# Retention's rotary half-swap: four ScalarE copies between partition halves in place of two matmuls with a constant matrix

## What is computed

```python
def apply_rotary(t, cos, sin):
    t1, t2 = jnp.split(t, 2, axis=-1)
    return jnp.concatenate([t1 * cos - t2 * sin, t1 * sin + t2 * cos], axis=-1)

def retention_mixer(q, k, v, cos, sin):
    q = apply_rotary(q.astype(f32), cos, sin)
    k = apply_rotary(k.astype(f32), cos, sin) * HEAD_DIM ** -0.5
    ...
```

## Time and profile before

| | us |
|---|---|
| median of 3 runs | 3160.13 |
| lowest and highest run | 3157.06 and 3163.06 |
| span of the profiled execution, first to last instruction | 3158.7 |
| TensorE busy in it | 3088.7 (98%) |
| VectorE busy | 1326.2 (42%) |
| ScalarE busy | 909.1 (29%) |
| GpSimd busy | 262.5 (8%) |

### The profile page before, as it was taken

The page is one execution under the profiler, slowest core; times in us unless marked ns, Lnnn a source line. Parts: engine busy times, 40 slices in busy tenths (PEclk is TensorE's granted clock), DMA queues, the critical chain, the costliest instruction groups (busy, mean ns, idle before and its releaser), DMA issues.

```text
span 3158.7 us, 35787 instructions
## 1 busy us (share of the span) xinstructions
PE 3088.7 (98%) x14698; PEld 2538.4 (80%) x14698; DVE 1326.2 (42%) x1417; ACT 909.1 (29%) x995; POOL 262.5 (8%) x275
## 2 busy tenths in 40 slices
PE   7999999999999999999899999999999999999998
PEld 5778777777789988887688888888888888888886
DVE  4534656555344442422324343334334343433335
ACT  6322433333344332322223212222221212122222
POOL 3000111100001123100022000000000000000002
PEclk8999999999999999999999999999999999999999
DMA  7333222222336764432433333332333333233332
GB/s 230 89 90 88 64 60 57 56 61 80 106 99 195 229 196 119 138 85 80 120 93 93 94 97 101 96 93 93 93 97 91 104 93 93 93 93 99 92 101 80
DMA packets 499007, 326.48 MB, mean 103 GB/s; under 512 B 12654, under 2 KB 487920, under 8 KB 498160
## 3 DMA queue, kind: packets, MB, share of 16 engines
q1 hardware_dynamic: 487568, 287.52, 32.1%
q0 software_dynamic: 11360, 37.85, 3.2%
HBM read 302.28 MB, written 23.07 MB: 103 GB/s over the span
## 4 chain that ended last, share of the span: by engine, by line
PE 92%; DVE 3%; ACT 3%; issue 1%; DMA 0%; POOL 0%; DVEq 0%; SPq 0%; ACTq 0%; POOLq 0%
PE slab_ps L652 20%; PE slab_ps L654 20%; PE slab_ps L653 20%; PE mix_ps L652 8%; PE mix_ps L654 8%; PE mix_ps L653 8%; PE mix_ps L1088 1%; PE mix_ps L1071 1%; PE mix_ps L821 1%; PE mix_ps L924 1%; PE mix_ps L829 1%; ACT w_hi L1167 1%; DVE w_lo L1650 1%; PE mix_ps L828 1%; PE mix_ps L966 1%
## 5 line engine op out<-in xcount | busy, mean ns | idle before, releaser
L652 PE MATMUL slab_ps<-act_hi,w_hi 128*128 128x512 f32 (+1 forms) x3216 | 1230.5, 383 | 13.4 <-DVE act_lo L2118 6.4
L654 PE MATMUL slab_ps<-act_hi,w_lo 128*128 128x512 f32 (+1 forms) x3216 | 1201.8, 374 | 0.0
L653 PE MATMUL slab_ps<-act_lo,w_hi 128*128 128x512 f32 (+1 forms) x3216 | 1201.5, 374 | 0.0
L1167 ACT ACTIVATE w_hi<-w_raw 128x2048 fp32r<-128x2048 f32 x264 | 505.2, 1914 | 1274.0 <-PE slab_ps L654 695.9
L652 PEld LDWEIGHTS slab_ps<-act_hi,w_hi 128*128 128x128 f32 x3216 | 608.5, 189 | 132.3 <-issue 18.0
L1650 DVE TENSOR_TENSOR w_lo<-w_raw,w_hi 128x2048 fp32r<-128x2048 f32 x264 | 604.7, 2291 | 238.5 <-ACT w_hi L1167 238.3
L654 PEld LDWEIGHTS slab_ps<-act_hi,w_lo 128*128 128x128 f32 x3216 | 607.9, 189 | 107.9
L653 PEld LDWEIGHTS slab_ps<-act_lo,w_hi 128*128 128x128 f32 x3216 | 609.0, 189 | 106.3 <-issue 6.2
L654 PE MATMUL mix_ps<-u_hi,w_lo 128*128 128x512 f32 x1024 | 404.5, 395 | 0.0
L652 PE MATMUL mix_ps<-u_hi,w_hi 128*128 128x512 f32 x1024 | 404.5, 395 | 0.0
L653 PE MATMUL mix_ps<-u_lo,w_hi 128*128 128x512 f32 x1024 | 404.4, 395 | 0.0
(11 more groups left out here) (347 smaller groups left out, 1744.3 us busy)
## 6 DMA issues: line engine op xcount, KB each, us to landing
w_raw<-in_w_mlp_up_dram SPq DMA_DIRECT2D x64, 1024.0 KB, 6.4
w_raw<-in_w_mlp_down_dram SPq DMA_DIRECT2D x64, 1024.0 KB, 5.3
w_raw<-in_w_in_dram SPq DMA_DIRECT2D x56, 1024.0 KB, 5.5
w_raw<-in_w_cross_kv_dram SPq DMA_DIRECT2D x32, 1024.0 KB, 6.3
w_raw<-in_w_mix_out_dram SPq DMA_DIRECT2D x16, 1024.0 KB, 5.9
w_raw<-in_w_cross_q_dram SPq DMA_DIRECT2D x16, 1024.0 KB, 5.9
w_raw<-in_w_cross_o_dram SPq DMA_DIRECT2D x16, 1024.0 KB, 5.9
main<-x_park POOLq DMA_DIRECT2D x8, 1024.0 KB, 6.0
```

What stands on the lines that cost most here:

```text
L652: mm(ps, wh, xh, start=first, stop=False)
L653: mm(ps, wh, xl, start=False, stop=False)
L654: return mm(ps, wl, xh, start=False, stop=last)
L1167: fn(w_hi[:, slot], w_raw[:, slot], ACT.Copy).then_inc(on["slab_hi"], 1)
```

## The change

The matrix `rot`, its set-up on POOL and the two matmuls a head are gone. ScalarE's part of a retention head begins instead with a wait for `slab_out` and four activations of type Copy, 64 partitions by 512 each, from one half of `stage` to the other half of `ret_t`, the one that lands in partitions 0 to 63 with scale -1. Each raises `ret_rot` by one. VectorE waits for the first two before the sine product of q and for all four before that of k, and makes the product in place in `ret_t`, from SBUF. TensorE keeps its waits and starts with the transposes.

```diff
@@ tiles @@
-            rot = sb("rot", [P, P])
@@ gpsimd @@
-            chain.link(nc.gpsimd.memset(rot[:], 0.0))
-            for m0, base, fill in ((0, -CH, -1.0), (CH, 0, 1.0)):
-                half = rot[:, m0:m0 + CH]
-                chain.put(nc.gpsimd.affine_select(out=half, in_=half, compare_op=ALU.not_equal, fill=fill, base=base,
-                                                  pattern=[[-1, CH]], channel_multiplier=1))
@@ tensor: retention(par) @@
-                q, k, v = (stage[:, par, t] for t in range(3))
+                v = stage[:, par, 2]
                 head_starts()
                 pe.wait_ge(on["slab_out"], slabs.at())
-                mm(M[0][:], rot[:], q, start=True, stop=True)
-                mm(M[1][:], rot[:], k, start=True, stop=True).then_inc(on["ret_rot"], 1)
                 turn(M[2], lambda t: v[:, t * P:(t + 1) * P], "vt_ready")
@@ scalar @@
-            def retention():
+            def retention(par):
                 head_starts()
+                act.wait_ge(on["slab_out"], slabs.at())
+                for n in range(2):
+                    fn(ret_t[0:CH, n], stage[CH:P, par, n], ACT.Copy, scale=-1.0).then_inc(on["ret_rot"], 1)
+                    fn(ret_t[CH:P, n], stage[0:CH, par, n], ACT.Copy).then_inc(on["ret_rot"], 1)
                 values(M[2])
@@ vector: retention(par, hd) @@
-                dve.wait_ge(on["ret_rot"], hd + 1)
                 for n, t in enumerate((q, k)):
                     dst = (ret_q, ret_k)[n]
                     chain.put(tt(dst[:], t, cos_t[:], ALU.mult))
-                    chain.link(tt(ret_t[:, n], M[n][:], sin_t[:], ALU.mult))
+                    dve.wait_ge(on["ret_rot"], hd * 4 + (2 * n + 2))
+                    chain.link(tt(ret_t[:, n], ret_t[:, n], sin_t[:], ALU.mult))
```

More of the change, by code:

```diff
@@ L1438, in _ @@
                 for par in range(2):
-                    mixer = retention()
+                    mixer = retention(par)
                     for _ in range(4):
```

## The result

The changed kernel takes **3198.06 us** (median of 4 runs, 3196.38 to 3198.27), the kernel before beside it 3158.6 us (4 runs, 3156.84 to 3163.06). The ratio is 1.0122, with a 95% interval of 1.011 to 1.0134: some 39 us slower, where 7 us less were forecast. The profiled execution took 3198.09 us, its span is 3196.6.

The account below looks back on a forecast made before the run. TensorE was taken to bound the kernel (busy 98%, 92% of the chain). Its -6.9 us, with 0 elsewhere, took the median from 3160.13 to 3153.2 us, range 3149.5 to 3159.0.

Parts of the forecast that it names:

- The step that failed: Stages behind retention: each was to start 6.9 us earlier and keep its shape.
- Removed matmuls, 6.9 us: TensorE in the four retention heads: losing two rotation matmuls saves 1.72 us a head, 6.9 us in all.
- The 3.5 us: Estimate for the removed matmuls' 16 records on TensorE by the skill's rule, about 216 ns each; set aside for measured distances.
- Junction 0: TensorE in retention heads: transposes now directly follow a slab's matmul, opening no gap, at most 0.1 us a head.
- Copies, 0.55 us each: ScalarE in retention heads: four added copies at 0.55 us each, 2.2 us a head, cost on the path 0.
- The cover: ScalarE in the second retention head: copies fit its 2.96 us idle before `vtok`, with 5.75 us idle later as second cover.
- VectorE's waits 0, 4.3 us of slack: VectorE in retention heads: waiting for copies before the sine products costs 0; sums stay 4.3 us ahead of TensorE's scores.
- POOL's set-up and the moved tiles, 0: Dropping POOL's memset and two selects (1.0 us) gains 0; tiles moving 512 bytes a partition without `rot` cost 0.
- C: Retention heads: slow copies hold VectorE's second wait and stop TensorE; at 3.2 us a copy, 3169.7 us; chance 0.03.
- if the stage is 6.9 us shorter and the end is not: Profile sign of a wrong forecast, for A or D; the granted clock behind 307 us was to tell which.
- A: Near delta heads' ends: shifted clock falls; two more in the median give 3156.6 us, two fewer 3149.8; chance 0.22.
- D: Unexamined slack, say in the delta heads, takes the shift back: nothing measurable, 3160 us; chance 0.07.

Follow-up runs that it names:

- e2: Kernel before without the two rotation matmuls a head and their waits, nothing in their place, half-swap left out, `rot` and set-up kept: 3197.9 us, ratio 1.0117.
- e1: Changed kernel with 32 already met waits (16 instructions) on TensorE ahead of the MLP's loop, putting it back to its old place: 3153.78 us, ratio 0.998.
- e4: Kernel before with one turn of the output projection's loop written out and 24 instructions of met waits ahead of the MLP's loop: 3182.56 us, ratio 1.0073.
- e6: Changed kernel with one turn of the cross-attention output projection's loop written out ahead of it, no waits added: 3151.53 us, ratio 0.9973.
- e3: Changed kernel with `rot`, its set-up and its two matmuls a head put back, results unused, VectorE still using the copies: 3161.5 us, ratio 1.0004.
- e7: e1 with 8 instructions of met waits in place of 16, so the MLP's loop starts at 12746: 3153.2 us.
- e8: e4 with 12 instructions of met waits in place of 24, so the MLP's loop starts at 12960: 3179.95 us.
- e10: e6 with 72 met waits (37 instructions) put inside the MLP's loop at its top, body 1615 instructions: 3203.55 us.
- e11: e4 with 36 instructions of met waits in place of 24, so the MLP's loop starts at 12984: 3188.66 us.

## Why the prediction was wrong

**The step that failed** is: "After retention every stage starts 6.9 us earlier and keeps its shape, since its weights are loaded into slots that TensorE and VectorE free." The stages behind retention have the same work and the same waits, but they didn't keep their place in TensorE's instruction stream. The prediction counted the eight matmuls as time where they stood and nothing else; without their 16 instructions the MLP's loop, which makes its first jump at 2069 us, begins ahead of a piece boundary instead of behind it. e2 makes this loss out of the removal alone, e1 takes it back with 16 instructions that do nothing, and e4 brings a loss of the same kind into the kernel before. The bill is -6.9 + 6 x 7.2 = +36, measured +39.

Term by term:

- *Removed matmuls, 6.9 us*: right. The first delta head starts 6.86 us earlier, and e1 (ratio 0.998, so 6.3 us less) and e6 (0.9973) show the gain at the end once the loop stays resident. The 3.5 us that the prediction worked out from the Trainium skill ("TensorE: Matmul & The Clock Gate", section "Back-to-back issue gap") was half of what came.
- *Junction 0*: right, 0.24 and 0.44 us.
- *Copies, 0.55 us each*: too low. The timeline of ScalarE in the second head, after:

```profile
149.18 1.92 ACT L1159 ACTIVATE w_hi<-w_raw 128x2048 fp32r<-128x2048 f32 x1 [8.96 <-PE slab_ps L648]
151.12 0.63 ACT L1288 ACTIVATE ret_t<-stage 64x512 f32<-64x512 f32 x1
151.77 0.63 ACT L1289 ACTIVATE ret_t<-stage 64x512 f32<-64x512 f32 x1
...
153.74 0.60 ACT L1182 ACTIVATE vtok<-mix_ps 128x512 f32<-128x512 f32 x1
...
154.89 0.63 ACT L1169 ACTIVATE gtmp<-gtmp 128x512 f32<-128x512 f32 x1
...
160.55 1.92 ACT L1159 ACTIVATE w_hi<-w_raw 128x2048 fp32r<-128x2048 f32 x1 [4.36 <-PE slab_ps L648]
```

  They start 0.65 us apart, each 0.63 long: as long as a pass of the sigmoid over 128 partitions beside them (L1169), so half the partitions made them no shorter and the way between halves no longer. Four take 2.6 us, where 2.2 was said. The cover was right: they lie in what was idle time ahead of `vtok`. They hold `vtok` back by about 1.5 us behind the transposes (done at about 152.2), as the prediction had it in kind, and nothing waited for it.
- *VectorE's waits 0, 4.3 us of slack*: right, and e3 shows it by itself. Timeline of VectorE there, after:

```profile
154.27 0.69 DVE L1759 TENSOR_TENSOR ret_t<-ret_t,sin_t 128x512 f32<-128x512 f32 x1
...
155.60 0.69 DVE L1759 TENSOR_TENSOR ret_t<-ret_t,sin_t 128x512 f32<-128x512 f32 x1
156.32 1.79 DVE L1760 TENSOR_TENSOR ret_q<-ret_q,ret_t 128x512 f32<-128x512 f32 x1
158.03 0.68 DVE L1761 TENSOR_TENSOR ret_k<-ret_k,ret_t 128x512 f32<-128x512 f32 x1
```

  No idle time stands at either product. The slow sum is now that of q, as said might be. The sums end at 158.03 + 0.68 = 158.7, and TensorE starts its scores at 163.02: 4.3 us.
- *POOL's set-up and the moved tiles, 0*: right. e1 has both and lands on the forecast; no run tried the set-up alone.
- *Rivals*: C, slower, was priced at 3169.7 through the copies, which had to take 2.2 us or more; they take 0.65. So the sign came from a mechanism that was not on the list. The sign "if the stage is 6.9 us shorter and the end is not" came true, but it was written down for A and D, and it was neither. A names the granted clock as a cause that strikes at random; here it fell as a consequence, in the same place of every turn. The views that were read hold engines, waits and the shares of DMA; the page's line of q8 with its 56 packets stood there and wasn't asked what fetches them and when they stop.

**What would have shown it.** From the kernel before: 56 packets of 256 instructions are 14336, about as long as TensorE's program without repeats (14480 in the built program), so the seven turns cost no fetch. Then the loop's length in pieces (1578 / 256 = 6.16) says that a body is slow if it starts more than 1792 - 1578 = 214 instructions behind a boundary, 41 places of 256, about one in six. The change moves the start by 16 instructions. Without knowing where the boundary lies, that alone is 16 in 215 that a fast loop becomes slow: a chance of some 7% for +40 us. The place of the boundary can't be read from the profile of before; e7 and the second stop found it. The kernel before has another loop close to the limit: that of the delta heads has 1708 instructions and starts at 1813, 76 behind a boundary, so it ends 8 short of an eighth piece, and from 454.45 to 633.14 us, where its second turn runs, q8 moves no packet.

**Open.** Why the packet ahead of the jump comes at e8's first three jumps and not at the last three. How much of e10's 7.0 us is its waits and how much the fetch. What the store does where the fetch doesn't run ahead: the runs show that seven pieces touched stay and eight don't. Why the profile puts the same kind of stop down to `issue` at one jump and to VectorE's L2204 at another wasn't tried.

## What to carry to other kernels

A loop on TensorE is part of the price list: count its body in instructions, against the 256 of a packet of the instruction queue, and after any edit ahead of it compare the packets of that queue in the page before comparing anything else. If a small edit costs several times what it touches, look for idle put down to `issue` at the loop's jumps; some met waits ahead of the loop, or a turn of an earlier loop written out, tell in one run whether the place does it, and repair it. A change should be judged with the loop in a fast place, else the place is measured and not the change.

## What was not expected of the hardware

- A loop body of 1578 instructions ran seven times from one fetch (56 packets in all); touching one piece more, it cost nine packets and 7.2 us a turn (110 packets), with 4.9 us of idle and the rest at the clock's 1.2 GHz level behind it.
- Between 56 packets and 110 lie 8 instructions of shift (start 12746 against 12738).
- The cost of a refetched turn depends on how the boundaries fall into the body: 3.6 us in e4 (3182.56 - 3161.11, by six), 4.6 in e11 (3188.66 against the same 3161.11), 7.8 in the changed kernel (3198.06 - 3151.53, by six) and 8.4 in e10 (3203.55 - 3153.42, by six, with the waits of its longer body in it).
- ScalarE's copy of 64 partitions by 512 between the partition halves took 0.63 us, 128x512 in the same place 0.63.
